# Routing weights of an expert layer: added into cells in memory by indirect DMAs, where one-hot products made them

## The chip, the cores and the metric

The program runs on one core of a Trainium2 chip. What is measured is the device time of one execution in microseconds; lower is better. Three runs of the kernel before took 2304.7, 2306.9 and 2309.52 us.

## What is computed

One inference step of a decoder layer in fp32, for 256 prompt tokens and 8 sample tokens (264 live ones, and 16 meta tokens in the first part). The first part is a combined input projection, stick-breaking attention, a convolution branch, two branch projections, gates and an output projection. The second part, where the change is, retrieves experts:

```python
s = einsum('chpk,pnk->chpn', (h @ w_query), sub_keys)         # 8 heads, two halves, 128 keys each
s1, i1 = top_k(s[:, :, 0], 16); s2, i2 = top_k(s[:, :, 1], 16)
top_s, pos = top_k(all 256 sums s1 + s2, 16)                   # 16 experts per token and head
idx = i1 * 128 + i2 at pos
gate = softmax(top_s)
act = gelu(einsum('cd,chkd->chk', h, expert_u[idx]))
out = einsum('chk,chkd->cd', gate * act, expert_v[idx])
```

There are 128 x 128 = 16384 experts, `expert_u` and `expert_v` have one row of 2048 numbers each. A final norm follows.

## The kernel before, in words

The kernel doesn't gather `expert_u` for each token. It multiplies all 16384 rows with all 264 tokens (the **up stage**), weighs the products with a mostly empty table W of routing weights, and multiplies with all of `expert_v` (the **down stage**). An expert is a cell (a, n) of the 128 x 128 grid: a is the partition, n the up tile. `W` is on chip as [128 partitions a, 128 tiles n, 232 tokens] (`TD = 232`). The last 32 tokens (`TG`) are dealt with by gathers of their own.

**Weights in halves.** All weights are streamed in quarters of [128, 512] into four ring slots `raw` (eight quarters) by SP (`load_half`). ScalarE rounds a quarter to a high part (`split_hi`), VectorE makes the low part (`split_lo`), TensorE multiplies hi by hi, hi by lo and lo by hi (`quarter_products`, 12 matmuls of 264 columns a quarter, 48 a tile). There are four buffers of hi and of lo, and both splits run three quarters ahead of TensorE (`AHEAD`). SP loads a quarter as soon as its slot has been split, so eight quarters ahead of that split.

**Pairs.** All tiles are counted in pairs of two. The up stage is pairs `PAIR_QRY` to `PAIR_U`: 64 pairs, 128 tiles, one tile per n. In its first 31 pairs (to `PAIR_R`) VectorE also makes the routing choices: three pairs for the sample tokens, then 28 splits for each of 8 heads, with the instructions of `top16` between the splits. In `PAIR_R` the softmax follows (`soft_first`, an exponential on ScalarE, `soft_second`), then the selection for the last 32 tokens (`sel_from_choices`), which SP writes out and reads back (`g_dram`, `gch`), and six transposes on TensorE of the chosen keys and weights to [choice, token].

**One-hot products.** From `PAIR_R + 2` on, 58 groups of four tokens make W. Per token VectorE compares the numbers 0 to 127 with the chosen second key and multiplies by the weight (`make`, `rhot`), ScalarE makes the one-hot of the first key (square, relu: `lhot`), and TensorE multiplies them: four matmuls of 256 columns (`group`), one group in each up tile. VectorE adds the high and low halves from PSUM into W (`keep`).

**Up products.** ScalarE's gelu writes each tile to `ust` (line 1682), GpSimd's queue spills it to `u_dram` (line 1660, 132 KB). The down stage needs W times the up products. SP reads them back four tiles at a time (`up_in`, `urg`, 464 KB, line 1600) and VectorE multiplies them into W (`times_up`, line 1946), four tiles ahead of use, through the whole of pass 0.

**Down stage.** Two passes of 128 chunks, one for each half of the model dimension. Per chunk ScalarE and VectorE split W's slice (`w_part`, lines 1700 and 1951) and two quarters of `expert_v`; TensorE does 16 matmuls. GpSimd's queue gathers the 32 up products per partition of the last tokens (line 1668, 32 DMAs of single elements) after the last spill, and then 64 times 128 rows of `expert_v` (line 1554), which VectorE accumulates (line 1957).

What sets the order is the order of the code in each engine's function (`experts_sync`, `experts_gpsimd`, `experts_scalar`, `experts_vector`, `experts_tensor`); semaphores hold them together. `halves` writes the down stage for ScalarE and VectorE and calls `between` after every chunk.

Of the kernel before, what the change touches and what calls it, by code (L numbers as in the profile page):

```python
# [25 lines left out]
P = 128  # L26
# [30 lines left out]
GT = 4  # L57
# [3 lines left out]
TT = 3  # L61
# [17 lines left out]
def program(nc, ctx, weights, xT, gains, u_tiles, expert_v, v_rows, cache_k, cache_v, stateT, page_table, sb_bias,  # L79
# [33 lines left out]
    ust = [place(f"ust{b}", at["rows"] + 1056 * b, [P, LIVE]) for b in range(2)]  # L113
    sums = place("sums", at["ust1"], [P, 2, TT, PH])
# [4 lines left out]
    poff = place("poff", at["same"], [P, 2])  # L119
# [57 lines left out]
    assert at["tri16_r"] <= 212800  # L177
# [21 lines left out]
    cT = place("cT", at["W"], [P, 2, TD])  # L199
    wT = place("wT", at["cT"], [P, 2, TD], F32R)  # L200
    lhot = place("lhot", at["wT"], [P, 2, GT, NK], F32R)
    rhot = place("rhot", at["lhot"], [P, 2, GT, 2, NK], F32R)
# [4 lines left out]
    assert at["gacc"] <= at["scratch"] and at["rhot"] <= at["scratch"]  # L207
# [9 lines left out]
    RT = 2  # L217
# [14 lines left out]
    assert offs[0] <= NK * LIVE  # L232
# [8 lines left out]
    dist = place("dist", at["scratch"], [P, GT, NK])  # L241
    assert at["whl1"] <= at["chosen"] and at["dist"] <= at["scratch"] + 8 * TT * PH * PK
# [8 lines left out]
    u_dram = nc.dram_tensor("u_spill", [NK, P, LIVE], F32, kind="Internal").ap()  # L251
    u_rows = u_dram.rearrange("n p (t o) -> (n p t) o", o=1)
    g_dram = nc.dram_tensor("g_spill", [TG, 3, PH * PK], F32, kind="Internal").ap()
# [150 lines left out]

    x_in = [sem(f"x_in{c}") for c in range(4)]
# [32 lines left out]
    GATE_TILES = 2 * (PAIR_IN - PAIR_GLU)  # L438
    PAIR_K = PAIR_Q + 1
# [49 lines left out]
    with nc.Block() as block:  # L489
# [35 lines left out]
        def _(pool):  # L525
# [4 lines left out]
            nc.gpsimd.memset(eps[:, 1:2], LN_EPS).then_inc(fill0, 1)  # L530
            nc.gpsimd.memset(ident[:], 0.0).then_inc(const_ready, 1)
# [84 lines left out]
        def _(act):  # L616
# [903 lines left out]
    u_free, u_out = [sem("u_free0"), sem("u_free1")], [sem("u_out0"), sem("u_out1")]  # L1520
    u_in, w_mul = [sem("u_in0"), sem("u_in1")], sem("w_mul")
    soft = sem("soft")
# [70 lines left out]
    def experts_sync(sp):  # L1593
# [5 lines left out]
        def up_in(m, h):  # L1599
            sp.dma_start(urg[:, h], u_dram[bass.ds(4 * m, 4), :, 0:TD].rearrange("n p t -> p n t"))\  # L1600
                .then_inc(u_in[h], 16)
# [637 lines left out]
```

## Time and profile before

| what | us |
|---|---|
| median of three runs | 2306.9 |
| lowest, highest | 2304.7, 2309.52 |
| span of the profiled execution | 2269.1 |
| TensorE busy in it | 2235.4 (99%) |
| VectorE busy | 1785.3 (79%) |
| ScalarE busy | 1314.6 (58%) |
| GpSimd busy | 281.4 (12%) |

The profiled execution has a span of 2269.1 us from its first to its last instruction; a run's time holds some 38 us around that (the run times are those of other executions, and lie within 0.2% of each other). Times of rows are counted from the span's start. The up stage lies between about 810 and 1585 us, the down stage after it. "Busy" of GpSimd is the time in which it makes the descriptors of its DMAs; the DMAs themselves run on 16 DMA engines that all queues share.

### The profile page before, as it was taken

The numbers are of one execution on the slowest core, as the hardware profiler recorded it, in microseconds if no ns is written. First come the engines' busy times: TensorE is split into PE (matmuls) and PEld (weight loads), VectorE is DVE, ScalarE is ACT, GpSimd is POOL, SyncE is SP. The second block draws the span as 40 slices with busy tenths as digits, with TensorE's granted clock in tenths as the row PEclk, the third lists the DMA queues.
The fourth block names the chain that finished last, engine by engine and source line by source line (L and its number), as shares of the span: only waits on it lengthen the run. The fifth ranks groups of instructions, "written<-read, shape, count | busy, mean of one in ns | idle before, by whom it ended". The sixth has DMA issues, their size and how long they took to land.

```text
span 2269.1 us, 58087 instructions
## 1 busy us (share of the span) xinstructions
PE 2235.4 (99%) x16784; PEld 2159.8 (95%) x16784; DVE 1785.3 (79%) x3359; ACT 1314.6 (58%) x2486; POOL 281.4 (12%) x338
## 2 busy tenths in 40 slices
PE   9999999999999999999999999999999999999997
PEld 8999899999999999999999999999999999999996
DVE  8787688887766667877878888886788898777786
ACT  6445365567454444444457777775555555555564
POOL 0321100002010000010000000000711122111110
PEclk9999999999999999999999999999999999999999
DMA  7887644455556556666656555556899998887874
GB/s 237 284 291 251 209 147 144 144 163 203 178 179 207 168 189 204 196 207 203 200 175 216 187 188 187 188 188 211 254 307 316 301 338 298 255 255 256 253 251 154
DMA packets 266522, 498.40 MB, mean 220 GB/s; under 512 B 32240, under 2 KB 55096, under 8 KB 266304
## 3 DMA queue, kind: packets, MB, share of 16 engines
q1 hardware_dynamic: 244256, 425.44, 58.8%
q0 software_dynamic: 22176, 71.89, 8.4%
q8 instruction: 40, 0.66, 0.1%
q14 instruction: 50, 0.41, 0.1%
HBM read 472.10 MB, written 25.11 MB: 219 GB/s over the span
## 4 chain that ended last, share of the span: by engine, by line
PE 74%; DVE 1%; ACT 1%; issue 1%; SPq 0%; DMA 0%; DVEq 0%; ACTq 0%
PE ps L2106 19%; PE ps L311 15%; PE ps L314 14%; PE ps L310 14%; PE ps L2110 10%; PE ps L2082 1%; ACT hi L293 0%; PE ps L1381 0%; DVE lo L298 0%; DMA raw<-u_tiles 0%; PE ps L2129 0%; DVE x L2059 0%; DVE yc L1419 0%; SPq L1610 0%; SPq L1609 0%
## 5 line engine op out<-in xcount | busy, mean ns | idle before, releaser
L298 DVE TENSOR_TENSOR lo<-raw,hi 128x512 fp32r<-128x512 f32 x1504 | 1019.5, 694 | 320.7 <-ACT hi L293 270.6
L293 ACT CAST hi<-raw 128x512 fp32r<-128x512 f32 x1504 | 921.6, 618 | 516.8 <-PE ps L314 422.8
L310 PE MATMUL ps<-h_hi,hi 128*128 128x264 f32 (+1 forms) x3200 | 820.9, 286 | 2.2 <-DVE h_lo L937 2.2
L311 PE MATMUL ps<-h_lo,hi 128*128 128x264 f32 (+1 forms) x3200 | 819.3, 286 | 0.0
L310 PEld LDWEIGHTS ps<-h_hi,hi 128*128 128x128 f32 x3200 | 602.0, 188 | 9.7 <-issue 6.0
L311 PEld LDWEIGHTS ps<-h_lo,hi 128*128 128x128 f32 x3200 | 602.4, 188 | 0.0
L314 PE MATMUL ps<-h_hi,lo 128*128 128x264 f32 (+1 forms) x3200 | 523.8, 286 | 7.1 <-DVE lo L298 7.0
L2106 PE MATMUL ps<-whl,hi 128*128 128x464 f32 x2048 | 516.0, 373 | 2.3 <-ACT half_sum L1744 1.5
L314 PEld LDWEIGHTS ps<-h_hi,lo 128*128 128x128 f32 x3200 | 444.2, 188 | 9.4 <-DVE lo L298 9.4
L2106 PEld LDWEIGHTS ps<-whl,hi 128*128 128x128 f32 x2048 | 347.7, 190 | 25.4 <-issue 3.0
L2110 PEld LDWEIGHTS ps<-whl,lo 128*128 128x128 f32 x2048 | 306.5, 190 | 22.3
L2110 PE MATMUL ps<-whl,lo 128*128 128x232 f32 x2048 | 309.3, 273 | 0.0
L1700 ACT CAST whl<-W 128x232 fp32r (+1 forms) x256 | 99.1, 387 | 177.0 <-PE ps L2110 177.0
L1660 POOL DMA_DIRECT2D u_spill<-ust x128 | 70.0, 547 | 808.9 <-ACT ust L1682 780.3
L1951 DVE TENSOR_TENSOR whl<-W,whl 128x232 fp32r<-128x232 f32 x256 | 102.0, 398 | 77.0 <-ACT whl L1700 76.4
L1554 POOL DMA_INDIRECT gat<-expert_v,gidx x64 | 95.7, 1496 | 492.6 <-DVE gacc L1957 492.0
L1045 DVE SCALAR_TENSOR_TENSOR yc<-cv,dw,yc 128x256 f32<-128x256 f32 x240 | 107.5, 480 | 0.1
L1682 ACT ACTIVATE ust<-ps 128x264 f32<-128x264 f32 x128 | 50.0, 391 | 80.9 <-PE ps L314 80.9
L1931 DVE SCALAR_TENSOR_TENSOR rhot<-iota,cT,wT 128x256 fp32r<-128x256 f32 x232 | 96.6, 479 | 0.0
L1957 DVE SCALAR_TENSOR_TENSOR gacc<-gat,gw,gacc 128x1024 f32<-128x1024 f32 x64 | 81.9, 1279 | 0.3 <-DMA gat<-expert_v,gidx 0.3
L1690 ACT ACTIVATE dist<-iota,cT 128x128 f32<-128x128 f32 x232 | 74.3, 391 | 4.1
L1940 DVE TENSOR_REDUCE W<-ps 128x1024 f32 (+1 forms) x58 | 70.7, 1218 | 0.0
(306 smaller groups left out, 1939.6 us busy)
## 6 DMA issues: line engine op xcount, KB each, us to landing
raw<-u_tiles SPq DMA_DIRECT2D x512, 256.0 KB, 3.0
raw<-expert_v SPq DMA_DIRECT2D x512, 256.0 KB, 6.0
raw<-weights SPq DMA_DIRECT2D x480, 256.0 KB, 3.0
u_spill<-ust POOLq DMA_DIRECT2D x128, 132.0 KB, 3.3
urg<-u_spill SPq DMA_DIRECT2D x32, 464.0 KB, 5.9
qb<-q_spill POOLq DMA_DIRECT2D x8, 512.0 KB, 6.4
x<-xT SPq DMA_DIRECT2D x4, 560.0 KB, 6.5
kvT<-qkv SPq DMA_DIRECT2D x1, 2240.0 KB, 10.9
```

Of the source, the lines that this page charges most:

```text
L293: nc.scalar.copy(hi[k % SPLIT][:], raw_quarter(k)).then_inc(hi_done, 1)
L298: nc.vector.tensor_tensor(lo[k % SPLIT][:], raw_quarter(k), hi[k % SPLIT][:].bitcast(F32), ALU.subtract).then_inc(lo_done, 1)
L310: pe.matmul(out, a, rhs[0][:, first + j, 0:n], start=start and j == 0, stop=False)
L311: pe.matmul(out, a, rhs[1][:, first + j, 0:n], start=False, stop=False)
L314: m = pe.matmul(out, lo[k % SPLIT][:, j], rhs[0][:, first + j, 0:n], start=False, stop=stop and j == QT - 1)
L1045: return nc.vector.scalar_tensor_tensor(out=yc[:, j, 0:SEQ], in0=cv[:, j, k + META:k + META + SEQ], scalar=dw[:, j, k:k + 1], in1=yc[:, j, ...
L1554: nc.gpsimd.indirect_dma_start(gat[n % 2][:], None, v_rows, bass.IndirectOffsetOnAxis(ap=index, axis=0)).then_inc(gat_in[n % 2], 16)
L1700: nc.scalar.copy(whl[k % 2][:, 0], W[:, chunk(i, k), :]).then_inc(whi_done, 1)
L1931: m = nc.vector.scalar_tensor_tensor(out=rhot[:, b, t], in0=spread(iota[:], 1, 2), scalar=cT[:, 1, tok], in1=wT[:, :, tok].bitcast(F32).br ...
L1951: nc.vector.tensor_tensor(whl[k % 2][:, 1], W[:, chunk(i, k), :], whl[k % 2][:, 0].bitcast(F32), ALU.subtract).then_inc(wlo_done, 1)
L2106: pe.matmul(ps[:, bank(QT * r + j), 0:2 * TD], a[:, j], whl[k % 2][:].rearrange("p a n -> p (a n)"), start=start, stop=False, skip_group_c ...
L2110: m = pe.matmul(ps[:, bank(QT * r + j), 0:TD], b[:, j], whl[k % 2][:, 0], start=False, stop=stop, skip_group_check=True)
```

## The change

The one-hot products, the six transposes and all that feeds them are gone. In their place:

- A table `w_dram` of 128 x 128 x 232 cells lies in memory. ScalarE's queue fills it with zeros in the gate stage, after every second gate tile: 16 DMAs of 8 tiles each (`zero_cells`).
- The softmax is done in four batches of two heads (`BATCH`), each as soon as its heads are chosen, between the splits (`soft_first`, `exp_weights`, `soft_second`); VectorE then computes the address of each choice's cell, ((second key) x 128 + first key) x 232 + token (`cells_of`).
- GpSimd adds the weights into the cells: per head, token tile and rank one indirect DMA with one element per partition and an add, 8 x 2 x 16 = 256 (`add_cells`). Of one token tile a head's adds wait for those of the head before it.
- The up products of the 232 tokens stay on chip: gelu writes them straight into `W`. Only the last 32 tokens' products are spilled, 16 KB a tile, now from SP's queue, behind loads of weights (`spill`).
- The last 16 up pairs (`PAIR_W` on, pair 48 of the stage): SP waits for all adds, then reads the cells back two times a pair (`cells_in`, 464 KB each), and VectorE multiplies the up products by them (`times_up`), all but the last group, which is multiplied after 24 chunks of pass 0. Pass 0 has no such loads or multiplications any more.

Core of the diff:

```diff
-    urg = place("urg", at["W"], [P, 2, 4, TD])
-    gacc = place("gacc", at["urg"], [P, 2, HALF * P])
-    gsel = place("gsel", Y, [P, 2, 2, PH * PK])
+    wld = place("wld", at["W"], [P, 2, 4, TD])
...
+    w_dram = nc.dram_tensor("w_spill", [NK, P, TD], F32, kind="Internal").ap()
+    w_cells = w_dram.rearrange("n p (t o) -> (n p t) o", o=1)
...
+            def zero_cells(m):
+                act.wait_ge(zeros_made, 1)
+                act.dma_start(w_dram[ZERO_N * m:ZERO_N * m + ZERO_N].rearrange("n p t -> p n t"),
+                              spread(zeros[:], 1, ZERO_N)).then_inc(w_zeroed, 16)
...
+                if t % 2:
+                    zero_cells(t // 2)
...
-    PAIR_G = PAIR_R + 2
+    BATCH = 2
+    BATCHES = PH // BATCH
+    PAIR_S = [PAIR_H + HEAD_SPLITS * BATCH * (b + 1) // 8 for b in range(BATCHES)]
+    SOFT = 5
+    CELLS = 16 * PH * PK
+    CHUNKS = NK // 4
+    PAIR_W = PAIR_U - CHUNKS // 2
...
+        def spill(i, b):
+            sp.wait_ge(tile_free[b], i + 2)
+            sp.dma_start(u_dram[2 * (i - PAIR_QRY) + b], ust[b][:]).then_inc(u_out[b], 16)
+
+        def cells_in(m, h):
+            sp.dma_start(wld[:, h], w_dram[bass.ds(4 * m, 4)].rearrange("n p t -> p n t")).then_inc(w_in[h], 16)
...
+                    if s == 1:
+                        spill(i - 2, 1)
+                    if s == 3:
+                        spill(i - 1, 0)
...
+        u_tiles_in(PAIR_R + 5, PAIR_W)
+        for t in range(RT):
+            sp.wait_ge(w_added[t], CELLS)
+        with sp.Fori(PAIR_W, PAIR_U) as i:
+            for s in range(RAW):
+                load_half(sp, 4 * i + s, s, u_tiles[4 * (i - PAIR_QRY) + s])
+                if s == 1:
+                    spill(i - 2, 1)
+                if s == 3:
+                    spill(i - 1, 0)
+            for h in range(2):
+                sp.wait_ge(w_mul, 2 * (i - PAIR_W) + h + 1)
+                cells_in(2 * (i - PAIR_W) + h, h)
...
         stream(1, 2)
-        for b in range(2):
-            sp.wait_ge(u_free[b], NK // 2 + 1)
-        sp.wait_ge(w_mul, 1)
-        up_in(2, 0)
+        spill(PAIR_U - 1, 1)
...
+        pool.wait_ge(w_zeroed, 16 * NK // ZERO_N)
...
-        with pool.Fori(0, NK // 2) as i:
-            for b in range(2):
-                pool.wait_ge(tile_free[b], i + PAIR_QRY + 2)
-                nc.gpsimd.dma_start(u_dram[2 * i + b], ust[b][:]).then_inc(u_out[b], 16)
-                pool.wait_ge(u_out[b], 16 * i + 16)
-                pool.sem_inc(u_free[b], 1)
...
+        def add_cells(hd, t, k):
+            n = P if t == 0 else TD - P
+            nc.gpsimd.indirect_dma_start(w_cells, bass.IndirectOffsetOnAxis(ap=widx[0:n, t, hd, k:k + 1], axis=0),
+                                         chosen[0:n, 2, t, hd, k:k + 1], None, compute_op=ALU.add)\
+                .then_inc(w_added[t], 16)
+        for hd in range(PH):
+            if hd % BATCH == 0:
+                pool.wait_ge(soft, SOFT * (hd // BATCH + 1))
+                pool.wait_ge(widx_made, RT * (hd // BATCH + 1))
+            for t in range(RT):
+                if hd:
+                    pool.wait_ge(w_added[t], 16 * PK * hd)
+                for k in range(PK):
+                    add_cells(hd, t, k)
...
+            n = 2 * (i - PAIR_QRY) + b
+            nc.scalar.activation(W[:, bass.ds(n, 1), :], ps[:, b:b + 1, 0:TD], ACT.Gelu_apprx_tanh)
+            act.wait_ge(u_out[b], 16 * (i - PAIR_QRY) + 1)
             act.sem_inc(act_go, 1)
...
-            nc.scalar.activation(ust[b][:], ps[:, b, 0:LIVE], ACT.Gelu_apprx_tanh).then_inc(tile_free[b], 1)
...
+            if isinstance(c, int) and c == 0:
+                act.wait_ge(w_mul, CHUNKS + 1)
+            if p == 0 and isinstance(i, int) and 8 * i + k == NK - 8:
...
+        def exp_weights(b):
+            act.wait_ge(soft, SOFT * b + 2)
+            w = chosen[:, 2, 0:TT if b == 0 else RT, BATCH * b:BATCH * b + BATCH]
+            nc.scalar.activation(w, w, ACT.Exp).then_inc(soft_act, 1)
...
+        for b in range(BATCHES):
+            up_pairs(ends[b] + 1, ends[b + 1])
+            up_pair(ends[b + 1], lambda k: exp_weights(b) if k == 2 else None)
+        up_pairs(PAIR_R + 1, PAIR_R + 5)
+        act.wait_ge(sel_out, SEL)
+        up_pairs(PAIR_R + 5, PAIR_U - 1)
+        up_pair(PAIR_U - 1, lambda k: w_part(0, 0, 0, 0) if k == 7 else None)
...
+        def cells_of(b):
+            heads = slice(BATCH * b, BATCH * b + BATCH)
+            first, second = (chosen[:, q, 0:RT, heads] for q in range(2))
+            if b == 0:
+                dve.wait_ge(poff_made, 1)
+            else:
+                dve.wait_ge(widx_made, RT * b)
+            nc.vector.tensor_scalar(wsum[:], second, float(P), None, ALU.mult).then_inc(cell_step, 1)
+            dve.wait_ge(cell_step, 2 * b + 1)
+            nc.vector.tensor_tensor(wsum[:], wsum[:], first, ALU.add).then_inc(cell_step, 1)
+            dve.wait_ge(cell_step, 2 * b + 2)
+            for t in range(RT):
+                nc.vector.tensor_scalar(widx[:, t, heads], wsum[:, t], float(TD),
+                                        part[:, 0:1] if t == 0 else poff[:, 2:3], ALU.mult,
+                                        ALU.add).then_inc(widx_made, 1)
+
+        for b in range(BATCHES - 1):
+            hooks[8 * PAIR_S[b], 5] = lambda b=b: soft_second(b)
+            hooks[8 * PAIR_S[b], 7] = lambda b=b: cells_of(b)
...
+                times_up(CHUNKS - 1, 1, CHUNKS // 2 - 1)
...
-            if p == 0 and k == 1:
-                times_up(i, 1)
-            if p == 0 and k == 5 and not (isinstance(i, int) and i == NK // 8 - 1):
...
+        lo_pairs(PAIR_R + 1, PAIR_R + 6)
+        idx_from_sel()
+        lo_pairs(PAIR_R + 6, PAIR_W)
+        dve.sem_inc(w_mul, 2)
+
+        def weighed(i, k):
+            h = k // 4
+            if h == 0:
+                for b in range(2):
+                    dve.wait_ge(tile_free[b], i + 1)
+            times_up(2 * (i - PAIR_W) + h, h, i - PAIR_W)
+        with dve.Fori(PAIR_W, PAIR_U - 1) as i:
             for k in range(8):
                 split_lo(dve, 8 * i, AHEAD + k)
...
+                if k in (1, 5):
+                    weighed(i, k)
...
-        pe_pairs(pe, PAIR_QRY + 1, PAIR_R + 1, h2, LIVE)
-        pe.wait_ge(soft, 5)
-        for t, n in ((0, P), (1, TD - P)):
-            for q in range(3):
-                m = pe.transpose(ps[:, 2 + q, P * t:P * t + n],
-                                 chosen[0:n, q, t].rearrange("p h k -> p (h k)"), ident[0:n, 0:n])
-        m.then_inc(tr_ready, 1)
-        pe_pairs(pe, PAIR_R + 1, PAIR_G, h2, LIVE)
...
-        def group(n, b):
-            pe.wait_ge(r_ready, n + 1)
-            pe.wait_ge(l_act, n + 1)
-            pe.wait_ge(g_used, n + 1)
-            for t in range(GT):
-                m = pe.matmul(ps[:, 2 + 2 * b + t // 2, 2 * NK * (t % 2):2 * NK * (t % 2) + 2 * NK], lhot[:, b, t],
-                              rhot[:, b, t].rearrange("p h n -> p (h n)"), start=True, stop=True)
-            m.then_inc(g_ready, 1)
...
-                    if 4 * c + r in G_AT:
-                        group(2 * p + c, c)
-        pe_pairs(pe, PAIR_G + GP, PAIR_U, h2, LIVE)
+        pe_pairs(pe, PAIR_QRY + 1, PAIR_U, h2, LIVE)
```

**TensorE, an up tile in the stretch of the one-hot products, before** (the second half of a tile's quarters; `rhot`, `lhot` are the one-hots):

```order
L314 MATMUL ps<-h_hi,lo_54 128x264 x4
L307 REGISTER_ALU
L310 MATMUL ps<-h_hi,hi_51 128x264
...
L311 MATMUL ps<-h_lo,hi_51 128x264
L314 MATMUL ps<-h_hi,lo_55 128x264 x4
L2078 ISA
L2082 MATMUL ps<-rhot,lhot 128x256 x4
L307 REGISTER_ALU
L310 MATMUL ps<-h_hi,hi_52 128x264
```

In the changed kernel no row has `rhot` or `lhot`, and the products of one quarter follow those of the one before it, as in the other up tiles.

**GpSimd's queue in the expert part of the changed kernel**, with the semaphores that each row waits for (`w_added0` and `w_added1` are the adds of the two token tiles):

```order
L1683 MEMSET chosen 128x3x128 [waits w_zeroed]
L1684 MEMSET gacc 128x2048
L1691 DMA w_spill<-chosen,widx 3801088x1 [waits widx_made,soft]
L1691 DMA w_spill<-chosen,widx 3801088x1 x31
L1691 DMA w_spill<-chosen,widx 3801088x1 [waits w_added0]
L1691 DMA w_spill<-chosen,widx 3801088x1 x15
L1691 DMA w_spill<-chosen,widx 3801088x1 [waits w_added1]
L1691 DMA w_spill<-chosen,widx 3801088x1 x15
L1691 DMA w_spill<-chosen,widx 3801088x1 [waits w_added0,widx_made,soft]
```

Before, this stretch of the queue held the 128 spills of 132 KB and nothing else.

**VectorE, the last 16 up pairs of the changed kernel** (`wld` holds the cells read back):

```order
L299 TENSOR_TENSOR lo_54<-raw,hi_50 128x512 [waits mm_done]
L2072 REGISTER_ALU
L1971 ISA [waits tile_free1,tile_free0]
L1973 ISA [waits w_in0]
L1973 TENSOR_TENSOR W<-W,wld 128x928
L297 REGISTER_ALU
L298 REGISTER_ALU [waits hi_done]
L299 TENSOR_TENSOR lo_55<-raw,hi_51 128x512 [waits mm_done]
```

The multiplication stood among the chunks of pass 0 before (line 1946, with `urg`); now it stands behind the second low part of every tile, and waits there for the load of the cells.

## Rows read from the trace of the kernel before

**Rows 1.** Page, busy time of each engine and share of the span.
```profile
PE 2235.4 (99%) x16784; PEld 2159.8 (95%) x16784; DVE 1785.3 (79%) x3359; ACT 1314.6 (58%) x2486; POOL 281.4 (12%) x338
```
**Rows 2.** Stretches: length, busy us (count) per engine, granted clock, DMA share, GB/s.
```profile
280.00:520.00 240.00, 234.16 (x1853) 219.78 (x1852) 196.10 (x367) 145.19 (x227) 5.51 (x7) 1.00 0.47 148
...
815.00:1177.00 362.00, 362.00 (x2978) 362.00 (x2977) 284.81 (x784) 176.59 (x313) 34.40 (x62) 1.00 0.64 203
1177.00:1198.00 21.00, 21.00 (x176) 21.00 (x175) 14.14 (x32) 12.84 (x27) 1.62 (x3) 1.00 0.45 141
1198.00:1560.00 362.00, 361.84 (x2982) 361.63 (x2981) 299.96 (x517) 268.31 (x570) 31.31 (x58) 1.00 0.59 191
...
1700.00:1800.00 100.00, 100.00 (x625) 93.21 (x624) 85.09 (x136) 59.56 (x117) 13.09 (x9) 1.00 0.93 313
```
**Rows 3.** Waits of TensorE, longest in total: us, times, longest.
```profile
PE ps L314 <- DVE lo L298: 7.0, 10, 3.0
PE ps L310 <- DVE h_lo L937: 2.2, 4, 1.0
```
**Rows 4.** TensorE in order of time: start us, us, instruction.
```profile
1182.68 0.76 PE L2072 MATMUL ps<-ident,chosen 128*128 128x128 f32 x6
1183.22 0.37 PE L310 MATMUL ps<-h_hi,hi 128*128 128x264 f32 x1
...
1197.91 0.64 PE L2082 MATMUL ps<-rhot,lhot 128*128 128x256 f32 x4
1198.38 0.29 PE L310 MATMUL ps<-h_hi,hi 128*128 128x264 f32 x1
```
**Rows 5.** Line 2082: duration ns min/median/max, first and last start.
```profile
L2082 PE MATMUL ps<-rhot,lhot x232: 278/282/294, 1197.9 to 1558.3; 128*128 128x256 f32 x116
```
**Rows 6.** Group of line 1682: busy us, mean ns, idle before, releaser.
```profile
L1682 ACT ACTIVATE ust<-ps 128x264 f32<-128x264 f32 x128 | 50.0, 391 | 80.9 <-PE ps L314 80.9
```
**Rows 7.** ScalarE, then VectorE, in order of time around the exponential.
```profile
1174.81 1.28 ACT L1712 ACT_TABLE_LOAD   x1
...
1177.17 0.69 DVE L298 TENSOR_TENSOR lo<-raw,hi 128x512 fp32r<-128x512 f32 x1 [1.65 <-ACT hi L293]
```
**Rows 8.** SP's queue in order of time: two issues.
```profile
1593.46 0.38 SPq L1600 DMA_DIRECT2D urg<-u_spill  x1
...
705.28 0.68 SPq L1259 DMA_DIRECT2D x_spill<-x  x1
```
**Rows 9.** Page, DMA issues: count, KB each, median us to landing.
```profile
raw<-u_tiles SPq DMA_DIRECT2D x512, 256.0 KB, 3.0
...
u_spill<-ust POOLq DMA_DIRECT2D x128, 132.0 KB, 3.3
urg<-u_spill SPq DMA_DIRECT2D x32, 464.0 KB, 5.9
```
**Rows 10.** GpSimd in order of time, 4 of the 32 gathers of single elements.
```profile
1593.03 1.29 POOL L1668 DMA_INDIRECT gu<-u_spill,gidx  x1 [0.15 <-issue]
...
1598.71 0.94 POOL L1668 DMA_INDIRECT gu<-u_spill,gidx  x1 [0.31 <-issue]
...
1601.24 1.65 POOL L1668 DMA_INDIRECT gu<-u_spill,gidx  x1 [0.30 <-issue]
...
1638.55 0.94 POOL L1668 DMA_INDIRECT gu<-u_spill,gidx  x1 [0.30 <-issue]
```
**Rows 11.** VectorE in order of time: a multiplication, and the first use of the gathers.
```profile
1600.95 1.12 DVE L1946 TENSOR_TENSOR W<-W,urg 128x928 f32 x1
...
1647.20 0.18 DVE L1965 TENSOR_TENSOR gw<-gu,gch 128x32 f32<-128x32 f32 x1
```
**Rows 12.** Gathers of rows, line 1554: page group, then ns min/median/max.
```profile
L1554 POOL DMA_INDIRECT gat<-expert_v,gidx x64 | 95.7, 1496 | 492.6 <-DVE gacc L1957 492.0
...
L1554 POOL DMA_INDIRECT gat<-expert_v,gidx x64: 939/1454/2057, 1639.8 to 2226.4; - x64
```
**Rows 13.** GpSimd's DMA queue, 1593 to 1639 us: packets, MB, share of 16 engines.
```profile
q0 software_dynamic: 920, 0.02, 1.4%
```
**Rows 14.** The same queue, 900 to 1100 us, spills alone.
```profile
q0 software_dynamic: 1635, 4.60, 6.0%
```

More of the change, by code:

```diff
@@ L56 @@
 SPARE_TILE = 80
-GT = 4
 TG = 32
@@ L60 @@
 PARTS = P // TG
-TT = 3
+TT, RT = 3, 2
 NEG_BIG = -3.0e38
@@ L112, in program @@
     early = at["cvec"]
-    ust = [place(f"ust{b}", at["rows"] + 1056 * b, [P, LIVE]) for b in range(2)]
-    sums = place("sums", at["ust1"], [P, 2, TT, PH])
+    total = place("total", at["rows"], [P, LIVE])
+    widx = place("widx", at["rows"], [P, RT, PH, PK], I32)
+    ust = [place(f"ust{b}", at["total"] + 4 * TG * b, [P, TG]) for b in range(2)]
+    wsum = place("wsum", at["ust1"], [P, RT, 2, PK])
+    sums = place("sums", at["wsum"], [P, 2, TT, PH])
     gch = place("gch", at["sums"], [P, 3, TG])
@@ L118, in program @@
     same = place("same", at["gu"], [P, TG])
-    poff = place("poff", at["same"], [P, 2])
+    poff = place("poff", at["same"], [P, 3])
     assert at["poff"] <= early
@@ L2019, in after_pass, with lo_pairs @@
                     lo_part(m + 1)
-        for i in (PAIR_R, PAIR_R + 1):
+        LAST = BATCHES - 1
+        for k in range(8):
+            split_lo(dve, 8 * PAIR_R, AHEAD + k)
+            if k == 0:
+                soft_first(LAST)
+            if k == 4:
+                soft_second(LAST)
+            if k == 5:
+                cells_of(LAST)
+            if k == 6:
+                sel_from_choices()
+        def lo_pairs(first, last):
+            with dve.Fori(first, last) as i:
+                for k in range(8):
+                    split_lo(dve, 8 * i, AHEAD + k)
@@ L2026, in experts_vector @@
-                if i == PAIR_R and k == 4:
-                    soft_second()
-                if i == PAIR_R and k == 5:
-                    sel_from_choices()
-                if i == PAIR_R + 1 and k == 0:
-                    transposed()
-                if i == PAIR_R + 1 and k in DVE_AT:
-                    make(DVE_AT.index(k), DVE_AT.index(k))
-        dve.wait_ge(sel_out, SEL)
-        with dve.Fori(0, GP - 1) as p:
-            i = p + PAIR_G
-            for k in range(8):
-                split_lo(dve, 8 * i, AHEAD + k)
-                if k in DVE_AT:
-                    b = DVE_AT.index(k)
-                    keep(2 * p + b, b)
-                    make(2 * p + 2 + b, b)
@@ L2043, in experts_vector @@
-        for i in range(PAIR_G + GP - 1, PAIR_U):
-            for k in range(8):
-                split_lo(dve, 8 * i, AHEAD + k)
-                if i == PAIR_G + GP - 1 and k in DVE_AT:
-                    keep(2 * GP - 2 + DVE_AT.index(k), DVE_AT.index(k))
-                if i == PAIR_G + GP and k == 1:
-                    idx_from_sel()
-                if i == PAIR_U - 1 and k == 4:
-                    dve.wait_ge(g_used, GROUPS + 2)
-                    times_up(0, 0)
+                if k in (1, 5):
+                    weighed(i, k)
@@ L2053, in experts_vector @@
+        for k in range(8):
+            split_lo(dve, 8 * (PAIR_U - 1), AHEAD + k)
+            if k == 1:
+                weighed(PAIR_U - 1, k)
         w_part(0, 0, 0, 0)
@@ L2134, in experts_tensor @@
         pe.wait_ge(acc_done, 5)
-        pe.matmul(ps[:, bank(0), 0:LIVE], ones[:], ust[0][:], start=True, stop=False)
+        pe.matmul(ps[:, bank(0), 0:LIVE], ones[:], total[:], start=True, stop=False)
         for j in range(HALF):
```

207 lines of the change are left out of this document (71 added, 136 removed).

## The prediction

> **What bounds the kernel now.** I read the page's busy line first: TensorE is busy 99% of 2269.1 us, VectorE 79%, ScalarE 58%, GpSimd 12% [rows 1]. Then the stretches of the up stage: from 815 to 1177 us TensorE is busy for all 362 us with 2978 matmuls, from 1198 to 1560 for 361.84 us with 2982 [rows 2]. Both rates are one matmul per 121.5 ns (362 / 2978), with or without the one-hot products among them. So a matmul that goes there is time that goes, and a wait of another engine counts only when it empties TensorE. The whole list of TensorE's waits gives 7.0 us on VectorE's low parts, and everything else 3 us or less [rows 3]. Clock and DMA don't bind: the granted clock is 1.00 in every stretch of rows 2, that is the 2.4 GHz level, and the DMA share there is 0.45 to 0.71.
>
> **What goes from TensorE.** 232 one-hot matmuls are removed, four after each of 58 up tiles. A group of four begins at 1197.91 and the next product at 1198.38, so 0.47 us [rows 4]. A second way: the first of the 232 starts at 1197.9, the last at 1558.3 [rows 5]. Less three matmuls within the last group (0.36) this is 360.0 us over 57 tiles, 6.32 us a tile; 48 plain matmuls at 121.6 ns are 5.84 us; the difference is 0.48 us. 58 x 0.48 = 27.8 us. The six transposes start at 1182.68 and the next product at 1183.22, 0.54 us [rows 4]. Together **-28.3 us**. Nothing else leaves TensorE: pass 0 and pass 1 of the down stage keep their matmuls, and in pass 0 TensorE is already busy for 100.00 of 100 us with a DMA share of 0.93 [rows 2], so its lighter VectorE (31 of 32 multiplications of 1.12 us [rows 11] leave it) and the 15 MB that it no longer reads buy nothing.
>
> **What is added, and what covers it.**
> - ScalarE, up stage: each up tile now has two activations, 232 and 32 columns wide, where it had one of 264 at 391 ns [rows 6]. Bounded by a second one of the same price that is +0.78 us in a pair of 11.7 us, while 58 squares-and-relu groups leave. ScalarE is 49% busy from 815 to 1177 [rows 2] (176.59 of 362). Cost 0.
> - Softmax in four batches: three more exponentials, each with two table loads of 1.28 us. The one that exists ran at 1174.81, the next high part came late and VectorE idled 1.65 us [rows 7], yet TensorE shows no wait there: 21.00 of 21 us busy [rows 2]. The new ones fall where VectorE also routes, 284.81 of 362 us busy (79%), so it has some 17 us to spare in the 82 us between two batches against about nine small instructions of 0.15 to 0.56 us. Cost 0, at worst 2 us a batch, 6 in all.
> - SP's queue: the 128 spills of up products move from GpSimd to SP, behind the weight loads (an issue is about 0.4 us [rows 8]), and are 16 KB in place of 132. By the code each waits for a tile whose activation stands before the split that the load ahead of it already waited for, so SP doesn't stop. The buffer is wanted back seven quarter-tiles later (7 x 1.46 = 10.2 us), the landing is 3.3 [rows 9]. Cost 0.
> - SP, last 16 pairs: 32 loads of 464 KB come in, two a pair. The first of a pair has about 6.5 us to land; it takes 5.9 in the crowded pass 0 [rows 9]. VectorE's multiplication is 1.12 us, two a pair, 2.2 on top of 5.5. TensorE holds four quarters, so a landing 2 us late still empties nothing. Bytes: 180 GB/s of weights plus 80 stays under the 313 of pass 0 [rows 2]. Cost 0.
> - Zeroing: ScalarE issues 16 DMAs of 0.95 MB in the gate stage (280 to 520). An issue of 464 KB in 512 rows takes SP 0.38, one of 2112 KB 0.68 [rows 8], so 6 to 11 us of ScalarE in 240; it is 60% busy and TensorE is idle only 5.8 us of 240 [rows 2], mostly on attention's chain. I take **+1 us**, between 0 and 5.
> - Junction to the down stage: the last spill can go only after the loads of chunks 4 to 7, at 1593.5 in old times [rows 8], and lands 3.3 us later [rows 9]. The 32 gathers behind it, 47 us, then end near 1644, where they ended at 1639.5 [rows 10]. VectorE wants them at 1647.2 [rows 11], and now has a 1.12 us multiplication there too. **+0.5 us**, between 0 and 3.
>
> **The adds themselves** are the unknown: no DMA of before adds in memory. GpSimd issues 256, 16 per head and token tile, 64 per batch, each of 128 (or 104) single elements. The nearest row is the gather of single elements: 32 in 45.5 us (1593.03 to 1638.55, 31 steps), **1.47 us apart** with the pause of 0.30 [rows 10]. The other bounds are the cheapest steps there, 1.24, and the slowest row gather, 2.06 plus 0.30 [rows 12]. I take 1.47, since it is the same size, kind and back-to-back issue. They may take long, since they start early. Batch 0 has its indices in pair 10 of the up stage, about 815.6 + 20.75 x 5.84 = 937 us; SP stops for the sum of them after the loads of pair 47, near 815.6 + 92 x 5.84 = 1353, and has a further 8 us, because a weight quarter is asked for 11.7 us ahead and lands in 3.0 [rows 9]. So 424 us are allowed and 256 x 1.47 = 376 wanted: **0, as long as one add costs under 424 / 256 = 1.66 us**. Last batch alone: 64 x 1.47 = 94 us after pair 31, with some 180 left, so a slow start during routing is made good later.
>
> A rule speaks against many such DMAs: the Trainium skill, "DMA: Bandwidth & Descriptors" (rules for kernel authors, and its anatomy of one DMA), says that transfers under 64 KB pay mostly overhead, about 2.0 us each. Taken per add, one behind the other, that gives by this page 512 us and 88 us of stall, about 2368. The trace disagrees for the gather: 1.47 us apart, the fixed part overlapping.
>
> Descriptor writing is also disturbed by VectorE. A gather that starts at 1601.24 takes 1.65 us beside the multiplication of 1600.95, the one at 1598.71 takes 0.94 [rows 10, 11]. The Trainium skill, "SBUF — State Buffer" (who interferes with whom), lets only copies, casts and scalar operations block descriptor generation, and infers that a two-input operation doesn't; by the row it costs up to 0.7 us, and the routing stage is full of those. 136 adds at 1.80 in the 245 us of routing and 120 at 1.47 after it are 421 us: still just in time.
>
> **Sum.** 2269.1 - 28.3 + 1.5 = 2242.3 of span. The span lies 37.8 us under the median of 2306.9 (the runs hold time around it), so the forecast is 2306.9 - 26.8 = **2280 us**. For itself this case runs from 2274 (no cost, a few stalls fewer) to 2286.
>
> **Rivals.**
> 1. *The adds don't drain in time* (slower). Adding needs a read of the target, so a descriptor may cost more than a gather's. It decides from 1.66 us per add on: SP stands before the loads of pair 48, TensorE runs dry once. At 1.80 us (the usual row gather, 1.50 + 0.30 [rows 12]) 461 - 424 = 37 us: 2317. At 2.36, 180 us: about 2460. For: the margin is 11% and VectorE disturbs. Against: the equal-sized gathers. Chance 0.15. By the rule on small transfers of the Trainium skill's page "DMA: Bandwidth & Descriptors" (rules for kernel authors), this rival would be the case.
> 2. *The adds crowd the 16 DMA engines* (slower). The gathers' queue shows 1.4% of the engines over 46 us, 0.3 us of engine time each [rows 13]. If every element cost what a spill's packet does, 6.0% x 16 x 200 us / 1635 = 117 ns [rows 14], one add is 128 x 117 / 16 = 0.94 us of all engines, 64% on top of the 64% that is used, and weights come late: 28% of 376 us, +105, near 2385. Chance 0.04.
> 3. *Cover is thin* (less gain). Table loads and index work push VectorE over in three batches (6), zeroing costs 5, the junction 3: 2306.9 - 28.3 + 14 = 2293; with late cell loads up to 2301. For: VectorE at 79% and idle gaps of 1 us. Chance 0.12.
> 4. *The removed matmuls buy nothing*, because the weight stream would then set the pace: 2307. Against: raw loads wait for free slots and ScalarE waits for TensorE, never long for them. Chance 0.03.
>
> **How the numbers follow.** The main case gets 0.66. Faster by over 0.2% (4.6 us, about what a measurement can tell): the main case and rival 3, 0.78. Within 0.2%: rival 4 and a mild rival 1, 0.05. Slower: 0.17. The range takes the main case, rival 3 and the mildest of rival 1: 2274 to 2305.
>
> **What would show it.** Right: no product of one-hots, matmuls from 815 us to the down stage about 770 - 28 = 742 us long with TensorE full, the 256 adds at about 1.5 us steps, the last of them well before pair 48, no wait of SP on them. Wrong: one gap of TensorE before the last 16 pairs (rival 1), weight loads that land in 6 us and more from 940 on (rival 2), TensorE waits on low parts near 940, 1020 and 1100 or between 280 and 520 (rival 3), an unchanged length of the stage with ScalarE waiting for raw loads (rival 4).

## Result and profile after

The changed kernel takes **2366.99 us** (median of 4, 2365.48 to 2368.26), the kernel before beside it 2308.21 (4 runs): ratio 1.0254, 95% interval 1.0239 to 1.0268. It is 59 us slower; the forecast was 2280, and the range ended at 2305. What happened is rival 1 of the prediction (the adds don't drain in time), with adds 1.99 us apart.

The page of the changed kernel, busy time, and three of its rows of 40 slices (59 us each):

```profile
PE 2217.7 (94%) x16546; PEld 2140.8 (91%) x16546; DVE 1648.7 (70%) x3097; ACT 1221.7 (52%) x2333; POOL 630.6 (27%) x467
...
PE   9999999999999999999999914999399999999997
...
PEclk9999999999999999999999957999699999999998
DMA  6887566665555556777788715887277788677774
```

TensorE has two holes, where the profile of before shows none [rows 1]. First its waits (us, times, longest), then the same stretches by busy time (length, busy us per engine, granted clock, DMA share, GB/s):

```profile
PE ps L311 <- ACT hi L294: 82.5, 1, 82.5
PE ps L2108 <- DVE whl L1978: 26.5, 4, 25.7
PE ps L2108 <- issue: 9.9, 1, 9.9
```
```profile
815.00:1340.00 525.00, 525.00 (x4314) 524.79 (x4313) 367.72 (x936) 268.20 (x552) 342.11 (x201) 1.00 0.74 183
1340.00:1450.00 110.00, 27.50 (x225) 27.30 (x224) 11.35 (x17) 11.63 (x25) 87.96 (x55) 0.63 0.29 30
1450.00:1655.00 205.00, 204.65 (x1633) 203.39 (x1633) 130.07 (x181) 103.08 (x215) 2.60 (x3) 0.99 0.82 263
1655.00:1705.00 50.00, 14.35 (x61) 12.73 (x60) 6.62 (x13) 5.89 (x12) 29.70 (x32) 0.58 0.23 71
1705.00:1900.00 195.00, 195.00 (x1209) 181.59 (x1209) 145.95 (x243) 115.22 (x227) 21.81 (x15) 0.99 0.76 245
```

**The first hole** is read in the chain of waits (start, us, what):

```profile
1441.08 1.60 POOL w_spill L1691
1442.98 3.07 DMA w_spill<-chosen,widx
1446.52 2.41 DMA raw<-u_tiles
1449.03 0.63 ACT hi L294
1449.70 0.59 PE ps L311
```

The last add is issued at 1442.98 and has landed at 1446.05; SP, which stood before the loads of pair 48, loads again, and TensorE goes on 3.6 us later. The line of the adds (ns min/median/max, first and last start):

```profile
L1691 POOL DMA_INDIRECT w_spill<-chosen,widx x256: 1545/1601/3456, 936.3 to 1443.0; - x128
```

(1443.0 - 936.3) / 255 = **1.99 us apart**: 1.60 of descriptor making (the median), 0.30 of pause, and 0.09 more in the mean, which lies mostly in the stretch of routing (below). The gathers it was costed by were 1.47 apart [rows 10].

**The second hole** lies under the 32 gathers of single elements (1651.79 to 1690.70). The profiled execution of before is full there (64.73 of 65 us busy from 1585 to 1650), so at first it looked like something new.

### The profile page after: what moved, and what is told of

Read it like the earlier page. It is cut to its first block and busy times, and to the rows that moved or that the text cites. A ratio compares the mean times of both kernels' runs of the same rounds, so it can differ in the third digit from the quotient of the medians.

```text
span 2365.4 us, 56301 instructions
## 1 busy us (share of the span) xinstructions
PE 2217.7 (94%) x16546; PEld 2140.8 (91%) x16546; DVE 1648.7 (70%) x3097; ACT 1221.7 (52%) x2333; POOL 630.6 (27%) x467
## 5 line engine op out<-in xcount | busy, mean ns | idle before, releaser
L299 DVE TENSOR_TENSOR lo<-raw,hi 128x512 fp32r<-128x512 f32 x1504 | 1030.8, 694 | 513.5 <-ACT hi L294 409.7
L311 PE MATMUL ps<-h_hi,hi 128*128 128x264 f32 (+1 forms) x3200 | 823.5, 286 | 83.7 <-ACT hi L294 82.5
L1691 POOL DMA_INDIRECT w_spill<-chosen,widx x256 | 430.1, 1680 | 307.8 <-DVE widx L1904 229.6
L1720 ACT ACTIVATE W<-ps 128x232 f32 (+1 forms) x128 | 46.6, 364 | 112.4 <-PE ps L315 95.1
L1707 POOL DMA_INDIRECT gu<-u_spill,gidx x32 | 30.4, 950 | 216.7 <-issue 216.7
L311 PE MATMUL ps<-raw_hi,hi 128*128 128x264 f32 x256 | 66.4, 289 | 0.0
L312 PE MATMUL ps<-mx_lo,hi 128*128 128x264 f32 x256 | 65.1, 285 | 0.0
```

The source lines that it names most:

```text
L299: nc.vector.tensor_tensor(lo[k % SPLIT][:], raw_quarter(k), hi[k % SPLIT][:].bitcast(F32), ALU.subtract).then_inc(lo_done, 1)
L311: pe.matmul(out, a, rhs[0][:, first + j, 0:n], start=start and j == 0, stop=False)
L312: pe.matmul(out, a, rhs[1][:, first + j, 0:n], start=False, stop=False)
L1691: nc.gpsimd.indirect_dma_start(w_cells, bass.IndirectOffsetOnAxis(ap=widx[0:n, t, hd, k:k + 1], axis=0), chosen[0:n, 2, t, hd, k:k + 1], N ...
```

## Experiments

The changed kernel is cut by the line numbers of its own file. "Late cells" below means: SP waits for the adds 10 pairs of tiles later. Each run is read against the kernel before as it ran on the same chip; these times matter from e12 on.

**e1, the kernel before again.**

> The kernel before, unchanged, profiled again. In the changed kernel TensorE works only 14.35 of the 50 us from 1655 to 1705, while the 32 gu gathers run one after the other (1651.79 to 1690.70), and its profiled span lies only about 2 us under its own time. The profiled execution of the kernel before has no such stall at its gathers (span 2269.1), though its own time was 37.8 us above its span. Theory A (ordinary executions of the kernel before have that stall too, and the one profiled had luck): either this profile shows about 36 us of TensorE idle between 1590 and 1660 and a span of about 2305, or again a span near 2269 beside a time near 2307. Theory B (the stall at the gathers is new with the change, and the 37.8 us lie outside the span): span near 2269 and no stall, in every profile. Time near 2307 in both.

2315.46 us (one run), span 2313.8. The longest waits of TensorE and the stretch of the gathers:

```profile
PE ps L2106 <- issue: 18.4, 4, 11.9
PE ps L2106 <- DVE whl L1951: 14.2, 5, 12.2
```
```profile
1585.00:1650.00 65.00, 34.42 (x188) 31.24 (x188) 21.82 (x37) 16.92 (x34) 36.70 (x37) 0.75 0.45 129
```

34.42 of 65 us, where the first profile has 64.73. This is theory A: the kernel before has the hole at its gathers too. From the last activation of the up stage to the end it takes 724.4 us here (2313.8 - 1589.4) and 684.1 in the first profile (2269.1 - 1585.0). So the 37.8 us between span and median in front of the prediction were this hole, and not time around the span (here 1.7).

**e2, half of the adds.**

```diff
-                for k in range(PK):
+                for k in range(PK if hd < PH // 2 else 0):
```

> The changed kernel with the adds of heads 0 to 3 only, 128 of 256 (the routing weights of heads 4 to 7 are left out of the cells). Theory 1 (the adds drain too late): the last add is issued before 1200, SyncE never waits, the stall of 82.5 us at 1366 to 1450 is gone, so about 2367 - 82.5 = 2284, and TensorE works 110 of 110 us from 1340 to 1450. Theory 2 (the loss is the crowd of small packets, or the weighing and the spills among the last tiles): the time stays above 2330.

2281.95 (2278.22 to 2285.86), ratio 0.9878 (0.9854 to 0.9902). The stretch of the first hole is full:

```profile
1340.00:1450.00 110.00, 110.00 (x906) 110.00 (x905) 65.28 (x89) 53.99 (x114) 0.00 (x0) 1.00 0.77 244
```

The 16 pairs with cell loads, multiplies and small spills cost TensorE nothing there: theory 1.

**e3, late cells.** Cells are read from pair 118 of the code's count on (pair 58 of the up stage, in place of 48); 12 of the 32 loads lie in the up stage, 20 in pass 0, where the kernel before had them.

```diff
-    PAIR_W = PAIR_U - CHUNKS // 2
+    UP_CHUNKS = 12
+    LATE_W = (CHUNKS - UP_CHUNKS) // 2
+    PAIR_W = PAIR_U - UP_CHUNKS // 2
...
         with sp.Fori(PAIR_W, PAIR_U) as i:
...
+            for t in range(RT):
+                sp.wait_ge(w_added[t], CELLS)
             for h in range(2):
...
+            if p == 0 and weighing[0] and k in (1, 5):
+                times_up(UP_CHUNKS + 2 * i + k // 4, k // 4, UP_CHUNKS // 2 + i)
```

> The changed kernel with all 256 adds, but the first cells are read back 10 pairs of tiles later (pair 118 in place of 108) and the last 20 of the 32 loads and multiplies lie among the first 80 chunks of the first down pass; SyncE waits for the adds behind the four loads of pair 118, where TensorE is due at about 1480. Theory 1 (only the place of the wait is wrong): adds still end at 1446, no stall there, 2284, plus at most 3 us if VectorE (78% busy in the first down pass) can't take 20 more multiplies of 1.2 us. Theory 2 (the adds themselves cost TensorE time by their packets or by GpSimd's port): clearly more than 2284, with pauses of TensorE spread over 940 to 1446. If the stall at the gu gathers depends on what else runs there, it may differ from 36 us here: its place is about 1575 to 1620.

2278.73 (2275.08 to 2283.25), ratio 0.9858 (0.9838 to 0.9879), with all 256 adds. From 1340 to 1450, 57 adds beside a full TensorE:

```profile
1340.00:1450.00 110.00, 110.00 (x907) 110.00 (x906) 52.27 (x76) 54.42 (x114) 92.92 (x57) 1.00 0.84 182
```

So the adds themselves take nothing from TensorE; what costs is where SP waits for them.

**e4, no element gathers** (on the changed kernel).

```diff
-        for j in range(TG):
-            nc.gpsimd.indirect_dma_start(gu[:, j:j + 1], None, u_rows,
...
+        nc.gpsimd.memset(gu[:], 0.0).then_inc(gu_in, 16 * TG)
```

> The changed kernel without the 32 gu gathers (gu is filled with zeros: the decode tokens' up products are left out). Theory A (the second stall comes from those gathers): the stall at 1655 to 1705 is gone, 2367 - 36 = 2331. Theory C (it comes from the turn from up tiles to down chunks, new loops whose code is not there yet, or from the x2 loads): the stall stays and the time is within 3 us of 2367.

2331.64 (2329.79 to 2335.21): 35 us less than the changed kernel. The first hole stays, the second is gone:

```profile
1655.00:1705.00 50.00, 50.00 (x313) 46.58 (x313) 33.34 (x59) 29.92 (x59) 2.74 (x3) 1.00 0.76 234
1340.00:1450.00 110.00, 29.80 (x246) 29.59 (x244) 12.39 (x18) 12.48 (x27) 91.75 (x58) 0.64 0.31 29
```

**e5, scatters that overwrite.**

```diff
-                                         chosen[0:n, 2, t, hd, k:k + 1], None, compute_op=ALU.add)\
+                                         chosen[0:n, 2, t, hd, k:k + 1], None)\
```

> The changed kernel with its 256 indirect DMAs overwriting cells in place of adding to them (a cell chosen by two heads holds one weight, not the sum). Theory 1 (the price of one add decides, and the stall goes away below 1.66 us each): if a plain scatter costs GpSimd what a gather of the same size does (0.94 + 0.30), the last is issued at about 936 + 256 x 1.24 = 1254, no stall at 1366, 2284; if the accumulation is free and element writes to memory cost the 1.60 + 0.30 in themselves, nothing changes, 2367. In between: each 0.1 us less per DMA takes 25.6 us off the stall.

2597.54 (2592.48 to 2599.3), ratio 1.1247: both branches of the expectation missed. A plain scatter is cheaper on GpSimd, and yet the kernel takes 231 us more than with adds:

```profile
L1691 POOL DMA_INDIRECT w_spill<-chosen,widx x256: 965/982/2138, 939.9 to 1503.9; - x128
```
```profile
1000.00:1200.00 200.00, 107.39 (x748) 101.62 (x749) 74.18 (x213) 48.23 (x100) 80.03 (x82) 0.71 0.27 81
```

The half-idle stretch is a mean of two things. The 64 scatters of a batch run from 939.9 to 1022.3 without a break; in the midst of them TensorE and the DMA engines stand, and between two batches TensorE is full:

```profile
960.00:1000.00 40.00, 6.55 (x18) 4.83 (x18) 2.11 (x7) 1.16 (x2) 30.55 (x32) 0.50 0.06 14
1040.00:1100.00 60.00, 60.00 (x496) 60.00 (x494) 50.00 (x142) 32.32 (x66) 0.00 (x0) 1.00 0.60 187
```

What ScalarE and VectorE waited for from 1100 to 1200, in the second batch:

```profile
ACT hi L294 <- remote: 71.4, 3, 33.0
DVE lo L299 <- remote: 70.3, 3, 32.7
```

These are waits of up to 33 us for nothing that the profile can name, as in the hole at the gathers (ScalarE up to 14.4 us in e1). While GpSimd issues small plain DMAs back to back, the rest of this core stops; beside the slower adds it doesn't.

**e6, paced gathers; e7, two at a time; e8, later gathers** (each on e3, the diffs in this order).

```diff
         for j in range(TG):
+            pool.wait_ge(mm_done, 2 * C0 + SPLIT + 4 * j // 3)
```
```diff
+            if j > 1:
+                pool.wait_ge(gu_in[j % 2], 16 * (j // 2))
```
```diff
+        pool.wait_ge(mm_done, 2 * C0 + 16)
         for j in range(TG):
```

> e3_late_cells with the 32 gu gathers paced by TensorE: gather j waits until the products of 1 + 2j/3 chunks of the down stage are done, so one each 1.7 us in place of one each 1.24 us. If the stall of about 37 us at the gathers comes from issuing them back to back, it is gone or much smaller: 2279 - 37 = 2242. If it comes from the gathers as such (each holds something up, whenever it is issued), 2279 or more. They end about chunk 22 of the 24 that are there before VectorE needs them, so a loss of up to 5 us from that side would be no surprise.

> e3_late_cells with at most two gu gathers under way: each waits until the one before the last has landed. Theory C (too many element gathers in flight choke the queues that the other transfers and the cores' code come through): the stall is gone or nearly, 2242 to 2260, if a gather lands within 2.5 us. Theory D (GpSimd's making of descriptors is what the others wait for): the stall stays in proportion to the time GpSimd works, 2279.

> e3_late_cells with all gu gathers moved behind the eighth chunk of the down stage (20 us later; VectorE's first use moves from chunk 24 to 32). Theory E (the stall is at the turn from up tiles to down chunks, where each engine leaves one loop for new code while the gathers run): the stall is gone, about 2242. Theories C and D: it moves with the gathers, 2279 within 3.

e6: 2254.64 (2250.89 to 2257.38), 24 of the expected 37 us. Of the rest, 9.1 is one wait that remains where the first twelve gathers came in a burst, 1.3 us apart:

```profile
PE ps L2134 <- DVE whl L2003: 9.9, 4, 9.1
```

e7: 2267.46 (2264.88 to 2269.72). No hole while the gathers run, but they end at 1641, 2.2 us apart, and VectorE waits for them; TensorE loses 22.2 us at that point:

```profile
PE ps L2136 <- DVE whl L2004: 22.9, 4, 22.2
```
```profile
1600.00:1620.00 20.00, 20.00 (x127) 18.66 (x126) 15.40 (x26) 11.78 (x23) 8.63 (x8) 1.00 0.83 263
```

e8: 2280.6 (2279.94 to 2282.24), unchanged. But its edit did not do what its expectation says. The line of the gathers in e3, then in e8:

```profile
L1731 POOL DMA_INDIRECT gu<-u_spill,gidx x32: 943/947/1427, 1573.3 to 1613.5; - x32
L1732 POOL DMA_INDIRECT gu<-u_spill,gidx x32: 943/947/1654, 1571.8 to 1613.2; - x32
```

The last activation of the up stage is at 1559.2 in e3 and 1554.9 in e8, so the gathers came 14.1 us behind it, and now 16.9: 2.8 us later and not 20. e8 decides nothing about theory E (the stop belongs to the turn to the down stage). What speaks against E is that the turn alone makes no hole (e4) and that e5 has its stops in the midst of the up stage. The theories C and D of e7 (too many DMAs in flight, GpSimd's making of descriptors) aren't told apart: pacing lowers both.

**e9, paced with room (on e3); e10, the same two edits on the kernel before.** VectorE's first use of the gathers moves to chunk 32 (`FIRST = 4`), and `pool.wait_ge(mm_done, 2 * C0 + SPLIT + 12 + 7 * j // 5)` (e10: `+ 6`).

> e3_late_cells with the gu gathers both paced (gather j waits for chunk 6 + 0.7 j of the down stage, one each 1.8 us) and given more room: VectorE's first use of them moves from chunk 24 to chunk 32, the gathered rows are then taken a little faster at the end of the first pass. e6_paced still lost about 9 us in TensorE from 1560 to 1600, where its first ten gathers came in a burst, and e7_two_open lost 22 us because the gathers ended after VectorE wanted them. With neither: 2254.6 - 9 = 2245 +- 3. If the gathers' 1.8 us spacing is still too dense: 2250 or more.

> The kernel before with nothing changed but the same pacing and room for its gu gathers. Theory A (its ordinary executions have the same stall of about 36 us at the gathers, and the one profiled had not): 2309 - 36 = 2273, and a span like the 2269.1 that was profiled. Theory B (the stall belongs to the changed kernels): 2309. The difference between this and e9 is then the change's own gain: 28 us if the sum of the prediction holds.

e9: **2246.5** (2244.16 to 2250.17), ratio 0.9737 (0.9723 to 0.975). e10: 2278.91 (2278.05 to 2282.43), ratio 0.987 (0.9855 to 0.9885). e9 is as expected, e10 is 6 us over its 2273. The gathers' stretch is full in e9 and, but for 1.2 us, in e10 (e9, then e10):

```profile
1570.00:1630.00 60.00, 60.00 (x376) 55.89 (x375) 45.04 (x77) 34.99 (x70) 35.54 (x34) 1.00 0.86 264
```
```profile
1590.00:1660.00 70.00, 68.81 (x429) 63.97 (x428) 51.72 (x87) 40.56 (x81) 39.23 (x36) 1.00 0.84 253
```

**e11, paced plain scatters** (e5 with `pool.wait_ge(mm_done, 8 * (PAIR_S[0] + 1) + SPLIT + PK * (RT * hd + t) + k)` before each).

> e5_plain_scatter with its 256 plain scatters paced by TensorE, one each 1.46 us in place of 1.28 (as there, a cell chosen by two heads holds one weight). If what stops all engines is the rate of GpSimd's small DMAs and 1.46 us is slow enough, the 315 us over 2284 are gone: 2284 (the last scatter goes at about 1320, before SyncE's wait). If the kind decides (adds to memory are harmless, plain transfers stop the rest whatever their rate), near 2597.

2309.8 (2306.68 to 2312.81): 288 of the 315 us are gone, so most of it is the rate and not the kind of DMA. The scatters are (1338.7 - 936.8) / 255 = 1.58 us apart in the mean, often two or three of them 1.3 apart and then a pause. The 2284 of the expectation was missed by 26: from 1000 to 1400 TensorE still lacks 12 of 400 us, and the up stage as a whole is 28 us longer than in e9.

**e12, seven heads of adds** (`hd < PH - 1`, `CELLS = 16 * (PH - 1) * PK`).

> The changed kernel with the adds of heads 0 to 6, 224 of 256 (the routing weights of head 7 are left out of the cells); all waits stay. If the adds drain in one line at 1.99 us each and SyncE waits for the last (theory 1), the last of them lands about 64 us sooner, at 1382, the stall shrinks from 82.5 to about 19 us and the time is 2367 - 64 = 2303. If part of the stall is a fixed cost of the wait (refilling the four buffers, the clock that fell), it is some us more: the edge above 2303 is that cost.

2268.15 (2262.35 to 2270.35), far from 2303, but on this chip the kernel before took 2271.09 (13 runs, 2268.4 to 2273.56) and not 2308. There are two kinds of chip, then: the first, on which the kernel before takes about 2308, and a second, on which it takes about 2271 (that it is the chip itself isn't proven; see the end). On the second the hole at the gathers is missing, in e12 by its trace (below), in the kernel before by its time; 2303 - 37 = 2266. The adds did what was expected: with 32 fewer the last is issued 57.7 us sooner (1385.3), which takes 60.3 us off the wait (82.5 to 22.2).

```profile
PE ps L311 <- ACT hi L294: 22.8, 2, 22.2
```
```profile
1595.00:1636.00 41.00, 41.00 (x257) 38.19 (x256) 27.50 (x49) 24.46 (x48) 31.55 (x32) 1.00 0.71 214
```

**e13, e14, e15: e3, e9 and e5 once more, on one chip.**

> The kernel of e3_late_cells again, beside e14 and e15 on one chip. If before takes about 2308 here, this takes 2279; if before takes about 2271 (a chip without the stall at the gathers), this takes 2271 - 27 = 2244, with TensorE full from 1560 to 1660.

> The kernel of e9_late_and_paced again. It should take 2246 on either kind of chip: 33 us under e13 where the stall is, and within 3 us of e13 where it is not.

> The kernel of e5_plain_scatter again (a cell chosen by two heads holds one weight). On a chip with the stall near 2597. On a chip without it nothing stops the other engines, its last scatter goes at about 1270, and it takes 2271 - 27 = 2244.

The chip was of the second kind: before 2271.98 (7 runs). e13 2246.62 (2243.5 to 2247.93), e14 2244.52 (2239.23 to 2245.94), e15 2244.08 (2241.44 to 2247.2); expected were 2244, 2246, 2244. The kernel with plain scatters took 2597.54 on a chip of the first kind and loses nothing here (stretch and line of e15, to be read against e5):

```profile
1000.00:1200.00 200.00, 199.99 (x1644) 199.78 (x1643) 156.94 (x434) 105.60 (x214) 155.61 (x137) 1.00 0.63 179
```
```profile
L1691 POOL DMA_INDIRECT w_spill<-chosen,widx x256: 965/1141/2322, 938.9 to 1313.8; - x128
```

**e16, the changed kernel again; e17, with paced gathers only.**

> The changed kernel, unchanged. On a chip where before takes about 2271: 2271 - 27 + 82.5 = 2326.5, with no stall at the gathers. On one where it takes about 2308: 2367 as before.

> The changed kernel with nothing new but the pacing of its gu gathers and their first use eight chunks later (as e9, e10). With the stall at the wait for the adds left alone: 2246.5 + 82.5 = 2329 on either kind of chip.

The chip was of the first kind (before 2309.8). e16: 2370.13 (2367.75 to 2373.14). e17: 2332.19 (2329.54 to 2337.09), 3 us over its 2329; its longest waits:

```profile
PE ps L311 <- ACT hi L294: 82.5, 1, 82.5
PE ps L315 <- DVE lo L299: 5.4, 10, 1.5
```

So 38 us of the changed kernel belong to its gathers. The hole has the same size in the kernel before, by the length of the down stage: 724.4 - 684.1 = 40 us there (e1 and the first profile), 726.4 - 687.1 = 39 between the changed kernel and e17. Yet pacing gave the kernel before only 29: e10's down stage is 692.3 us long, and why it isn't 684 isn't shown. The difference of the two paced kernels, 2332.19 - 2278.91 = 53 us, therefore comes out below the change's own loss; their up stages, which hold it, differ by 827.4 - 769.1 = 58 us.

## Why the prediction was wrong

**The step that failed** is "I take 1.47, since it is the same size, kind and back-to-back issue". A plain scatter of that size is indeed 1.47 apart: (1313.8 - 938.9) / 255 in e15. An add isn't: GpSimd needs 1.60 us for it (median) where a scatter takes 0.98 undisturbed (e5) and 1.14 in e15, and with the pause that is 1.90, above the 1.66 at which the forecast turned. The adds so became the path that TensorE waits on, where the prediction had put them at nothing. The thought stood in rival 1 ("adding needs a read of the target, so a descriptor may cost more") with a chance of 0.15, and its formula was good: 256 x (1.99 - 1.66) = 84 us, measured 82.5 of wait, and 85 in the length of the stage (below), which holds the refill and the lower clock too (granted clock 0.63 from 1340 to 1450). Added to the forecast of 2280 it gives 2364 or 2365, measured 2367. The nearest row was of another operation, and a margin of 11% didn't carry a chance of 0.66.

By the Trainium skill, "DMA: Bandwidth & Descriptors" (rules for kernel authors, and its anatomy of one DMA), I had 2.0 us per add and 2368; it deserved a larger chance than 0.15. The numbers agree, 1.99 and 2367, but by luck and not for its reason: single gathers and scatters of the same bytes follow each other 1.25 to 1.47 us apart, and an add lands 3.07 us after its issue while others are in flight, so no fixed time stands between one add and the next. What stands there is GpSimd's own 1.60 + 0.30.

**Disturbance by VectorE** was over-rated. 119 adds between 936 and 1177, in the midst of routing, took 204.24 / 119 = 1.72 us each, 73 between 1198 and 1340 took 1.64, against 1.60 undisturbed. The prediction had put 0.33 on each in routing; it was 0.12. The Trainium skill, "SBUF — State Buffer" (who interferes with whom), infers that two-input operations don't block descriptor making; for the adds the trace nearly agrees, 0.12 us.

**What held.**

- The removed matmuls. The first and last activation of the up stage (e10, the paced kernel before, then e9; the changed kernel last):

```profile
L1683 ACT ACTIVATE ust<-ps x128: 380/392/394, 819.4 to 1588.5; 128x264 f32<-128x264 f32 x128
```
```profile
L1745 ACT ACTIVATE W<-ps x128: 358/365/368, 813.3 to 1555.6; 128x232 f32 x116, 128x232 f32<-128x232 f32 x12
```
```profile
L1720 ACT ACTIVATE W<-ps x128: 358/364/367, 811.8 to 1639.0; 128x232 f32 x116, 128x232 f32<-128x232 f32 x12
```

  769.1 us before, 742.3 without the wait: -26.8, where the forecast had 770 to 742 (-28.3). With the wait it is 827.2, 85 more. In all, -27 + 85 = 58 of the 59 us. e2 and e3, which don't have the first hole, take 2281.95 and 2278.73: the 2280 of the forecast.
- Times by chunk and place: first add at 936.3 (forecast 937), SP's last load before the wait at about 1352 (forecast 1353), TensorE dry at 1449.7 - 82.5 = 1367 (forecast 1361).
- What was costed at 0 showed no cost: TensorE is busy 525.00 of 525 us from 815 to 1340 with three more softmax batches and the spills on SP; 204.65 of 205 with two cell loads a pair (landing 4.5 us). Zeroing, costed at 1, shows no loss of TensorE: 234.21 of 240 us from 280 to 520 in e2 against 234.16 [rows 2].

```profile
w_spill<-zeros ACTq DMA_DIRECT2D x16, 928.0 KB, 6.2
wld<-w_spill SPq DMA_DIRECT2D x32, 464.0 KB, 4.5
```
- Rival 2 (crowded DMA engines) didn't happen, though its cost was no fancy. The two queues from 1200 to 1300, with 52 adds:

```profile
q1 hardware_dynamic: 13310, 19.08, 63.0%
q0 software_dynamic: 7471, 0.03, 21.3%
```

  0.213 x 1600 / 52 = 6.6 us of engine time an add, 44% of rival 2's 15 (0.94 of all 16). The share of all queues stood at 0.84 and TensorE was full.

**A step that was wrong without harm**: that the span lies 37.8 us under the median because "the runs hold time around it". A run holds 2 us around its span. The profiled execution and the timed ones differed by the hole at the gathers. The sum was made as a difference, and that hole is in both kernels, so the error dropped out. That was luck: nothing in the prediction asked whether the time outside the span was the same after the change.

## What to carry to other kernels

Price a DMA by its operation, not by its size: an indirect add took GpSimd 1.60 + 0.30 us where a gather or scatter of the same 128 elements took 0.94 to 0.98 + 0.30 undisturbed. When a slow producer fills a table, put the wait where the table is first needed, and behind the transfers that don't need it: with the wait 10 pairs later the same change gives 1.4% (e3) instead of costing 2.5%. Keep GpSimd's small plain DMAs apart when other work runs, at some 1.8 us each in the mean; it cost nothing on the one chip without the hole where it was tried (e14, against e13) and gave 29 us to the kernel before (e10). And compare the span of a profile with the time of the very execution that was profiled, here 2 us apart, before time is put down as lying around it.

The version that beats both kernels is e9: 2246.5 against 2308.01, and 2244.52 against 2271.98 on the other kind of chip.

## What was unexpected

- **Chips differ.** The experiments ran on six chips. The kernel before took 2308.01 to 2309.8 on four chips and 2271.09 and 2271.98 on two, 7 to 15 runs each that agree within 0.4%. Nearly all of it is the hole at 32 element gathers: with these paced the same kernel takes 2246.5 and 2244.52 on the two kinds (e9, e14), back to back 2278.73 and 2246.62 (e3, e13). The first profile of before (span 2269.1) is of the second kind, its timed runs of the first. The same code with 256 plain scatters takes 2597.54 or 2244.08. That it is the chip and not something that goes with it isn't proven: no chip came twice.
- **All other engines stop**: ScalarE and VectorE wait up to 33 us for something that the trace puts down as remote or as issue, and four of SP's issues took 69.89 us (e5, from 1123.30), with the 16 DMA engines nearly idle (share 0.06 from 960 to 1000). A mean spacing of 1.76 us (e9, two or three 1.3 to 1.6 apart and then a pause), two at a time (e7, 2.2 us) or the accumulating form (1.90) avoids it; 1.58 (e11) mostly. Which shared part it is stays open.
- An accumulating DMA uses much more of the DMA engines than a plain one: 6.6 us of engine time for 128 elements, against 0.016 x 3200 / 137 = 0.37 us in e15, whose queue from 1000 to 1200 shows:

```profile
q0 software_dynamic: 4351, 0.08, 1.6%
```
